# First attention reordered: score, transpose and norm work moved by one slab, key norm between a value slab's tiles

## The chip, the cores and the metric

The kernel runs on one core of a Trainium2 chip. The metric is device time in microseconds; the shown time is the median of three runs.

## The reference

Input is x (256 tokens, 1024 features). The first block is a Mamba-2 mixer, a convolutional FFN, a differential attention with 8 heads, and a second FFN. A second block (an attention over selected keys, a recurrent unit, gates and an FFN) follows. The change touches only the differential attention:

```
k, v = split(rms_norm(x, kv_ln) @ kv_w)      # k: 8 heads x 2 x 64, v: 8 heads x 128
k = rms_norm(k, k_norm) ; q = rms_norm(rms_norm(x, attn_ln) @ q_w, q_norm)
p = softmax(q k^T / 8 + bias[head], causal)  # one for each of the two halves c = 0, 1
attn = p[c=0] - lam * p[c=1]
o = rms_norm(attn @ v, subln) * (1 - lam_init)   # per head
x = x + o @ attn_out_w
```

## The kernel before

All activations stay on chip, features on the partitions. Weights stream through as slabs of 1 MB: SyncE loads a slab into one of three buffers (`raw`), ScalarE rounds it to a high part (`split_hi`, L385, called by `hi`, L1046), VectorE subtracts to get the low part (`split_lo`, L394, called by `lo`, L1424), and TensorE forms three products per tile (high x low, low x high, high x high; `mm3`, issued at L628). `hi(name)` and `lo(name)` work two slabs ahead of the one named, and `hi` waits until TensorE has finished the slab that used the same buffer. In the attention `lo` also runs an `ada` reduction (L1440) ahead of its split and another behind it; each reads a 256 KB block that GpSimd loads into one of two buffers. This is work for the second block that is placed in this stretch.

Every engine has one instruction stream, executed in order, and engines meet only at semaphores. The order of the attention is therefore written out by hand, four times, and the four have to fit: in the plan (L134), on TensorE (L915), on ScalarE (L1283) and on VectorE (L1863). The plan gives each result in PSUM a group number; group g uses bank g mod 6, and TensorE may write it (`acquire`, L358) only when the group six places earlier has been given back by its reader.

The loop variable s runs over pairs of heads: k, q and v each have four slabs, s = 0 to 3, and slab s holds heads 2s and 2s+1. The small steps of a pair are:

- `kss`, `qss`: sums of the squares of k and q per head and token (L855 to L711 on TensorE), root on ScalarE (`head_rms`, L1252), inverse on VectorE (`inverse_rms`, L1778).
- `kr`: the inverse key norm spread over the features by TensorE (`inverses`, L876, matmuls at L733) and multiplied on VectorE (`head_norm`, L1790). The query norm is a factor of the scores (`q_norm`).
- `sc`: scores of a head, two halves (L900, L901), negated with the bias and reduced to row minima on VectorE (L1811 to L1819), exponentials on ScalarE (`exps1`, L1258), combined on VectorE (`combine`, L1844 to L1856).
- `at`, `pv`: transposes of the combined map (L890), copied by ScalarE (L1271), then the product with v (L910, L912), whose square and copy ScalarE takes (L1274, L1275).
- `os`, `or`: the same norm for the output of a pair (L711, root L1252, inverse L1778, spread L733, product L1790), then its high part on ScalarE (`output_high`, L1281) and its low part on VectorE (`output_low`, L1806).

ScalarE's exponential and root need different tables, which an instruction of its own loads (ACT_TABLE_LOAD). `keep_busy(n)` (L704) issues n matmuls into a bank that nobody reads. After the last pair the output projection `ao` (four slabs) begins, whose k-th step waits for the k-th head's low part.

The order before, on TensorE, for s = 1 to 3: slab k; of earlier pairs `or`, attention 2s-3; scores 2s-2; slab q; scores 2s-1; `kss`; slab v; `kr`; two fillers; attention 2s-2; `qss`; `os`. What is left of the last pairs runs after v3 with no slab beside it.

## Time and profile before

| | us |
|---|---|
| median of three runs (1316.74 to 1323.26) | 1320.35 |
| the profiled execution's own time | 1323.19 |
| span from its first to its last instruction | 1321.1 |
| TensorE busy | 1230.6 (93%) |
| VectorE busy | 934.0 (71%) |
| ScalarE busy | 723.3 (55%) |
| GpSimd busy | 56.7 (4%) |

The mean granted TensorE clock is 0.97. A busy TensorE is not TensorE at its peak, since matmuls are pipelined. In the profile the attention lies between 475 and 613 us from the span's start: the first slab k0 starts at 467.01, k1 at 493.35, k2 at 521.53, k3 at 551.45, and the first matmul of `ao` at 612.96. A row of a timeline gives the start, the duration, the engine, the line, the operation, what it writes and reads, its shape, how many like it follow each other (x), and in brackets the idle time before it with what ended it. Durations of matmuls in such rows overlap; the distance between starts is what TensorE spends.

### The profile page before, as it was taken

How to read it: one execution, taken by the hardware profiler on the slowest of the kernel's cores; microseconds unless marked ns; L12 is line 12 of the kernel's file. 1: busy time of each engine (PE TensorE's matmuls, PEld its weight loads, DVE VectorE, ACT ScalarE, POOL GpSimd, SP SyncE). 2: the span in 40 equal slices, each digit the busy share in tenths (PEclk: the TensorE clock that was granted, in tenths of full speed). 3: DMA queues.
4: the chain of work that ended last, by engine and by line, in shares of the span. 5: the costliest groups of instructions: out<-in, count | busy, mean ns of one | idle time of the engine just before them, and what ended most of it. 6: DMA issues, size and time to landing. Idle time of an engine off the chain costs nothing.

```text
span 1321.1 us, 24735 instructions
## 1 busy us (share of the span) xinstructions
PE 1230.6 (93%) x9546; PEld 1184.6 (90%) x9546; DVE 934.0 (71%) x1686; ACT 723.3 (55%) x1073; POOL 56.7 (4%) x115
## 2 busy tenths in 40 slices
PE   6998888999999988888999999899889899999997
PEld 5998787899999988878999999899878799999997
DVE  4977987688877677665887866549755576887743
ACT  4765665365664355554666542546874436666631
POOL 1000000100001101100000001000000000000000
PEclk9899998999999999989999999899999999999999
DMA  6545453655556745522455457443322343555450
GB/s 251 179 158 173 143 204 113 230 181 173 188 183 234 257 168 189 182 97 75 167 189 188 176 207 261 171 160 108 127 85 96 128 160 128 196 186 191 151 199 32
DMA packets 38417, 220.75 MB, mean 167 GB/s; under 512 B 4943, under 2 KB 7488, under 8 KB 16960
## 3 DMA queue, kind: packets, MB, share of 16 engines
q1 hardware_dynamic: 27504, 189.97, 40.9%
q0 software_dynamic: 8112, 26.75, 5.8%
q10 hardware_dynamic: 2720, 2.90, 0.7%
q8 instruction: 57, 0.93, 0.3%
q14 instruction: 24, 0.20, 0.0%
HBM read 218.49 MB, written 1.11 MB: 166 GB/s over the span
## 4 chain that ended last, share of the span: by engine, by line
PE 62%; DVE 18%; ACT 10%; DMA 6%; issue 3%; DVEq 0%; POOL 0%; ACTq 0%
PE ps L628 56%; DMA ada_w<-in_w_ada 6%; DVE wl L399 4%; ACT wh L392 3%; DVE ada_w L1440 1%; DVE work L1474 1%; DVE xl L1468 1%; PE ps_idle L704 1%; DVE small L1819 1%; PE ps L817 1%; DVE work L1701 1%; DVE work L1813 1%; DVE work L1615 1%; DVE work L1646 1%; DVE work L1950 1%
## 5 line engine op out<-in xcount | busy, mean ns | idle before, releaser
L628 PE MATMUL ps<-xh,wl 128*128 128x256 f32 x1784 | 515.3, 289 | 13.2 <-DVE wl L399 9.8
L628 PE MATMUL ps<-xl,wh 128*128 128x256 f32 x1784 | 509.7, 286 | 0.0
L628 PE MATMUL ps<-xh,wh 128*128 128x256 f32 x1784 | 509.5, 286 | 0.0
L399 DVE TENSOR_TENSOR wl<-raw,wh 128x2048 fp32r<-128x2048 f32 (+1 forms) x178 | 400.9, 2254 | 133.9 <-ACT wh L392 133.9
L628 PEld LDWEIGHTS ps<-xh,wl 128*128 128x128 f32 x1784 | 347.8, 195 | 20.5 <-DVE wl L399 11.1
L392 ACT ACTIVATE wh<-raw 128x2048 fp32r<-128x2048 f32 (+1 forms) x178 | 333.7, 1878 | 57.5 <-PE ps L628 48.4
L628 PEld LDWEIGHTS ps<-xl,wh 128*128 128x128 f32 x1784 | 347.7, 195 | 0.5 <-issue 0.2
L628 PEld LDWEIGHTS ps<-xh,wh 128*128 128x128 f32 x1784 | 347.4, 195 | 0.0
L628 PE MATMUL ps<-actr,wh 128*128 128x256 f32 x1888 | 341.1, 283 | 0.0
L628 PEld LDWEIGHTS ps<-actr,wh 128*128 128x128 f32 x1888 | 295.0, 192 | 0.1
L628 PE MATMUL ps<-actr,wl 128*128 128x256 f32 x944 | 269.2, 285 | 7.2 <-DVE wl L399 4.7
L628 PEld LDWEIGHTS ps<-actr,wl 128*128 128x128 f32 x944 | 181.5, 192 | 10.0 <-DVE wl L399 5.9
L1586 DVE SCALAR_TENSOR_TENSOR work<-ps,vecs,work 128x255 f32<-128x255 f32 (+1 forms) x336 | 144.5, 476 | 50.7 <-ACT work L1225 41.7
L1225 ACT ACTIVATE work<-ps,vecs 128x256 f32<-128x256 f32 x132 | 74.2, 564 | 140.6 <-PE ps L628 140.3
L1057 ACT ACTIVATE work<-x 128x256 f32<-128x256 f32 x56 | 22.4, 418 | 137.0 <-DVE x L1519 42.9
L1440 DVE CUSTOM_DVE_ANT_0 ada_w<-ada_w,cact 128x512 f32<-128x512 f32 x96 | 65.2, 686 | 43.6 <-DMA ada_w<-in_w_ada 43.3
L605 POOL DMA_DIRECT2D ada_w<-in_w_ada x96 | 51.9, 541 | 748.5 <-DVE ada_sum L1440 747.6
L704 PE MATMUL ps_idle<-tri,ident 128*128 128x256 f32 x250 | 64.1, 399 | 0.0
L704 PEld LDWEIGHTS ps_idle<-tri,ident 128*128 128x128 f32 x250 | 47.0, 199 | 6.8 <-issue 1.5
L1258 ACT ACTIVATE work<-work,small 128x128 f32<-128x128 f32 (+1 forms) x48 | 21.5, 450 | 31.0 <-DVE small L1819 31.0
L1216 ACT ACTIVATE work<-work 128x256 f32<-128x256 f32 x66 | 26.6, 403 | 3.6 <-DVE work L1586 3.6
L1753 DVE TENSOR_TENSOR actr<-work,actr 128x256 f32 (+1 forms) x66 | 27.6, 419 | 0.5 <-ACT actr L1221 0.2
(252 smaller groups left out, 1045.5 us busy)
## 6 DMA issues: line engine op xcount, KB each, us to landing
raw<-in_up SPq DMA_DIRECT2D x66, 1024.0 KB, 4.9
ada_w<-in_w_ada POOLq DMA_DIRECT2D x96, 256.0 KB, 4.3
raw<-in_xbc SPq DMA_DIRECT2D x12, 1024.0 KB, 5.1
raw<-in_z SPq DMA_DIRECT2D x8, 1024.0 KB, 6.7
raw<-in_so SPq DMA_DIRECT2D x8, 1024.0 KB, 6.7
raw<-in_dn0a SPq DMA_DIRECT2D x8, 1024.0 KB, 5.5
raw<-in_dn1a SPq DMA_DIRECT2D x8, 1024.0 KB, 5.4
raw<-in_dn2a SPq DMA_DIRECT2D x8, 1024.0 KB, 4.9
```

The costliest lines, as they stand in the source:

```text
L392: nc.scalar.activation(wh[:, b % RING, 0:n], raw[:, b % RING, 0:n], ACT.Copy).then_inc(hi_done, 1)
L399: nc.vector.tensor_tensor(wl[:, b % RING, 0:n], raw[:, b % RING, 0:n], wh[:, b % RING, 0:n].bitcast(F32), ALU.subtract).then_inc(lo_done, 1)
L605: pool.dma_start(ada_w[:, a % ARING, :], io["w_ada"][a // 2][:, 512 * (a % 2):512 * (a % 2) + 512])\
L628: mm = nc.tensor.matmul(o, l, r, start=start and n == 0, stop=stop and n == 2)
L704: nc.tensor.matmul(ps_idle[:, 0:T], ident[:, :], tri[:, 0:2, :].rearrange("p a b -> p (a b)"), start=True, stop=True)
L1057: A(sq[:, m % 2, :], x[:, m, :], ACT.Square).then_inc(sq_done, 1)
L1216: A(gsil[:, (j - 1) % RING, :], pre[:, 2 * ((j - 1) % RING), :], ACT.Silu)\
L1225: A(pre[:, 2 * (j % RING) + t, :], bank(tile_group(up, j, t))[:, 0:T], ACT.Identity, scale=vdyn(f"up_w{f}", 88 + 2 * s + t), bias=vdyn(f"u ...
L1258: A(lg[:, cols], lg[:, cols], ACT.Exp, scale=-1.0, bias=mins[:, q, row + i:row + i + 1], accum_out=sums_[:, row + i:row + i + 1]).then_inc ...
L1440: V.tensor_tensor_reduce(out=w, in0=w, in1=cact[:, 512 * half:512 * half + 512], scale=1.0, scalar=0.0, op0=ALU.mult, op1=ALU.add, accum_o ...
L1586: return V.scalar_tensor_tensor(dst[:, d:T], src[:, 0:T - d], w, dst[:, d:T], ALU.mult, ALU.add)
L1753: V.tensor_tensor(dst, hbuf[:, (j - 2) % RING, :], src.bitcast(F32), ALU.subtract)\
```

## The change

It writes the four orders anew, one loop over s = 0 to 3 and a tail written out. On TensorE slab s is now: k; scores 2s-1; `os` of pair s-2; q; attention 2s-2; `kss`; `qss`; first tile of v; `kr`; second tile of v; `or` of pair s-2; attention 2s-1; scores 2s. The tail is scores 7, `os` 2, six fillers, attention 6, `or` 2, attention 7, `os` 3, two fillers, `or` 3. To place `kr` between the tiles, `stream_tok` takes a function that it calls after tile 0. The fillers inside the loop are gone, and those of the tail go from 16 to 8. ScalarE and VectorE follow in the orders of the diff; no instruction of theirs is added or removed.

```diff
@@ -131,31 +131,34 @@
     pl.stream("dn0", 12, PAIR3)
     pl.misc("n2", 2)
 
-    for s in range(6):
-        if s < 4:
-            pl.stream(f"k{s}", 1, TWO)
-        if s >= 3:
-            pl.misc(f"or{s-3}", 2)
+    for s in range(4):
+        pl.stream(f"k{s}", 1, TWO)
+        if s:
+            pl.misc(f"sc{2*s-1}", 2)
         if s >= 2:
-            pl.misc(f"at{2*s-3}")
-            pl.misc(f"pv{2*s-3}")
-        if 1 <= s < 5:
-            pl.misc(f"sc{2*s-2}", 2)
-        if s < 4:
-            pl.stream(f"q{s}", 1, TWO)
-        if 1 <= s < 5:
-            pl.misc(f"sc{2*s-1}", 2)
-        if s < 4:
-            pl.misc(f"kss{s}")
-            pl.stream(f"v{s}", 1, TWO)
-            pl.misc(f"kr{s}", 2)
-        if 1 <= s < 5:
+            pl.misc(f"os{s-2}")
+        pl.stream(f"q{s}", 1, TWO)
+        if s:
             pl.misc(f"at{2*s-2}")
             pl.misc(f"pv{2*s-2}")
-        if s < 4:
-            pl.misc(f"qss{s}")
+        pl.misc(f"kss{s}")
+        pl.misc(f"qss{s}")
+        pl.stream(f"v{s}", 1, TWO)
+        pl.misc(f"kr{s}", 2)
         if s >= 2:
-            pl.misc(f"os{s-2}")
+            pl.misc(f"or{s-2}", 2)
+        if s:
+            pl.misc(f"at{2*s-1}")
+            pl.misc(f"pv{2*s-1}")
+        pl.misc(f"sc{2*s}", 2)
+    pl.misc("sc7", 2)
+    pl.misc("os2")
+    pl.misc("at6")
+    pl.misc("pv6")
+    pl.misc("or2", 2)
+    pl.misc("at7")
+    pl.misc("pv7")
+    pl.misc("os3")
     pl.misc("or3", 2)
     pl.stream("ao", 4, TWO)
     pl.misc("n3", 2)
@@ -682,7 +685,7 @@
 
                 repeat(pe, n, stage, rolled=kind == TWO, between=between, late=late)
 
-            def stream_tok(name, X):
+            def stream_tok(name, X, between):
 
                 for s in range(PL.N[name]):
                     b = PL.S[name] + s
@@ -697,6 +700,8 @@
                                      (X[0][:, k, P * t:P * t + P], X[1][:, k, P * t:P * t + P]),
                                      k == 0, k == KD - 1, True)
                         mm.then_inc(half_done if t == 0 else slab_done, 1)
+                        if t == 0:
+                            between()
 
             def keep_busy(n):
 
@@ -912,35 +917,38 @@
                 nc.tensor.matmul(bank(g)[:, P:T], vt[:, 1, P * h:P * h + P], ATt[:, h % 2, T:384],
                                  start=False, stop=True).then_inc(misc_done, 1)
 
-            for s in range(6):
-                if s < 4:
-                    stream(f"k{s}", (xh, xl), x_ready(2) if s == 0 else None)
-                if s >= 3:
-                    inverses("or", s - 3, orms, orinv_done, 1)
+            def output_sums(s):
+                sums_by_token("os", s, o_squares, ones[:, 0:1])
+
+            def output_inverses(s):
+                inverses("or", s, orms, orinv_done, 1)
+
+            for s in range(4):
+                stream(f"k{s}", (xh, xl), x_ready(2) if s == 0 else None)
+                if s:
+                    scores(2 * s - 1)
                 if s >= 2:
-                    attend(2 * s - 3)
-                if 1 <= s < 5:
-                    scores(2 * s - 2)
-                if s < 4:
-                    stream(f"q{s}", (x2h, x2l), x_ready(3) if s == 0 else None)
-                if 1 <= s < 5:
-                    scores(2 * s - 1)
-                if s == 4:
-                    keep_busy(3)
-                if s < 4:
-                    sums_by_token("kss", s, k_squares, halves)
-                    stream_tok(f"v{s}", (xh, xl))
-                    inverses("kr", s, krms, krinv_done, 2)
-                if 1 <= s < 5:
-                    keep_busy(9 if s == 4 else 2)
+                    output_sums(s - 2)
+                stream(f"q{s}", (x2h, x2l), x_ready(3) if s == 0 else None)
+                if s:
                     attend(2 * s - 2)
-                if s < 4:
-                    sums_by_token("qss", s, q_squares, halves)
-                if s >= 4:
-                    keep_busy(2)
+                sums_by_token("kss", s, k_squares, halves)
+                sums_by_token("qss", s, q_squares, halves)
+                stream_tok(f"v{s}", (xh, xl), lambda: inverses("kr", s, krms, krinv_done, 2))
                 if s >= 2:
-                    sums_by_token("os", s - 2, o_squares, ones[:, 0:1])
-            inverses("or", 3, orms, orinv_done, 1)
+                    output_inverses(s - 2)
+                if s:
+                    attend(2 * s - 1)
+                scores(2 * s)
+            scores(7)
+            output_sums(2)
+            keep_busy(6)
+            attend(6)
+            output_inverses(2)
+            attend(7)
+            output_sums(3)
+            keep_busy(2)
+            output_inverses(3)
             stream("ao", (oh, ol), lambda k: pe.wait_ge(ol_done, k + 1))
             ffn(1, "n3", 4, 3)
 
@@ -1280,37 +1288,39 @@
                     act.wait_ge(on_done, h + 1)
                     A(oh[:, h, :], qf[:, h, :], ACT.Copy).then_inc(oh_done, 1)
 
-            for s in range(6):
-                if s < 4:
-                    kq_tiles("k", s, kf)
-                if s >= 3:
-                    output_high(s - 3)
-                if s >= 2:
-                    attend(2 * s - 3)
-                if 1 <= s < 5:
+            for s in range(4):
+                if s:
                     exps1(2 * s - 2)
-                if s < 4:
-                    kq_tiles("q", s, qf)
-                if 1 <= s < 5:
+                kq_tiles("k", s, kf)
+                if s:
                     exps1(2 * s - 1)
-                if s < 4:
-                    head_rms("kss", s, krms, 8, 64)
-                    name = f"v{s}"
-                    hi(name, 0)
-                    for t in range(2):
-                        g = PL.G[name] + t
-                        wait_tile(act, name, 0, 0, t)
-                        A(vt[:, t, 256 * s:256 * s + 256], bank(g)[:, 0:256], ACT.Copy).then_inc(vt_done, 1)
-                        act.wait_ge(vt_done, 2 * s + t + 1)
-                        act.sem_inc(free[g % PRING], 1)
-                if 1 <= s < 5:
+                kq_tiles("q", s, qf)
+                if s:
                     attend(2 * s - 2)
-                if s < 4:
-                    head_rms("qss", s, qrms, 8, 64)
                 if s >= 2:
                     head_rms("os", s - 2, orms, 4, P)
-                if s == 5:
-                    output_high(3)
+                head_rms("kss", s, krms, 8, 64)
+                head_rms("qss", s, qrms, 8, 64)
+                name = f"v{s}"
+                hi(name, 0)
+                for t in range(2):
+                    g = PL.G[name] + t
+                    wait_tile(act, name, 0, 0, t)
+                    A(vt[:, t, 256 * s:256 * s + 256], bank(g)[:, 0:256], ACT.Copy).then_inc(vt_done, 1)
+                    act.wait_ge(vt_done, 2 * s + t + 1)
+                    act.sem_inc(free[g % PRING], 1)
+                if s >= 2:
+                    output_high(s - 2)
+                if s:
+                    attend(2 * s - 1)
+            exps1(6)
+            exps1(7)
+            head_rms("os", 2, orms, 4, P)
+            attend(6)
+            output_high(2)
+            attend(7)
+            head_rms("os", 3, orms, 4, P)
+            output_high(3)
             residual("ao", 3, 4, tiles_two("ao"))
             ffn(1, "n3", [4], {}, 3, ("ao", 3))
 
@@ -1860,31 +1870,35 @@
                     else:
                         step.add(ins)
 
-            for s in range(6):
-                if s < 4:
-                    lo(f"k{s}", 0)
-                if s >= 3:
-                    head_norm("or", s - 3, qf, sgs, on_done)
-                    output_low(s - 3)
-                if 1 <= s < 5:
-                    scores(2 * s - 2)
-                if s < 4:
-                    lo(f"q{s}", 0)
-                if 1 <= s < 5:
+            def output_norm(s):
+
+                head_norm("or", s, qf, sgs, on_done)
+                output_low(s)
+
+            for s in range(4):
+                lo(f"k{s}", 0)
+                if s:
                     scores(2 * s - 1)
                     combine(2 * s - 2)
-                if s < 4:
-                    inverse_rms("kss", s, krms, krinv_done)
-                    lo(f"v{s}", 0)
-                if 1 <= s < 5:
+                lo(f"q{s}", 0)
+                if s:
                     combine(2 * s - 1)
-                if s < 4:
-                    head_norm("kr", s, kf, vec("k_norm"), kqn_done)
-                    q_norm(s)
+                lo(f"v{s}", 0)
+                inverse_rms("kss", s, krms, krinv_done)
+                q_norm(s)
                 if s >= 2:
                     inverse_rms("os", s - 2, orms, orinv_done)
-            head_norm("or", 3, qf, sgs, on_done)
-            output_low(3)
+                head_norm("kr", s, kf, vec("k_norm"), kqn_done)
+                if s >= 2:
+                    output_norm(s - 2)
+                scores(2 * s)
+            scores(7)
+            combine(6)
+            inverse_rms("os", 2, orms, orinv_done)
+            combine(7)
+            output_norm(2)
+            inverse_rms("os", 3, orms, orinv_done)
+            output_norm(3)
             residual("ao", 3, 4, tiles_two("ao"))
             ffn(1, ("n3", [(4, lambda m: vec("ffn_ln1", m), None)], 3, ("ao", 3)), 3)
```

## Rows read from the trace of the kernel before

**Rows 1.** The page: busy time, and the last chain's shares by engine.

```profile
PE 1230.6 (93%) x9546; PEld 1184.6 (90%) x9546; DVE 934.0 (71%) x1686; ACT 723.3 (55%) x1073; POOL 56.7 (4%) x115
...
PE 62%; DVE 18%; ACT 10%; DMA 6%; issue 3%; DVEq 0%; POOL 0%; ACTq 0%
```

**Rows 2.** Windows: stretch, length; busy PE, PEld, DVE, ACT, POOL (count); clock, DMA share, GB/s.

```profile
493.35:521.53 28.18, 24.51 (x205) 22.79 (x205) 19.61 (x47) 16.82 (x36) 3.23 (x6) 1.00 0.53 180
521.53:551.45 29.92, 26.79 (x220) 24.76 (x220) 21.96 (x55) 19.08 (x43) 3.95 (x7) 1.00 0.51 175
576.90:612.96 36.06, 27.47 (x152) 22.98 (x153) 18.75 (x56) 16.64 (x43) 1.17 (x2) 0.81 0.13 44
```

**Rows 3.** Timeline of TensorE, slab s=1 from q1 on.

```profile
500.12 0.38 PE L628 MATMUL ps<-actr,wl 128*128 128x256 f32 x1
...
506.07 0.50 PE L900 MATMUL ps<-work 64*128 64x128 f32 x4
...
506.93 1.05 PE L711 MATMUL ps<-blk,work 128*128 128x2 f32 x8
...
516.84 1.09 PE L733 MATMUL ps<-ident,work 128*64 128x128 f32 x16 [3.00 <-DVE work L1778]
...
517.86 1.13 PE L704 MATMUL ps_idle<-tri,ident 128*128 128x256 f32 x4
...
519.99 0.67 PE L910 MATMUL ps<-work 128*128 128x256 f32 x2 [0.67 <-ACT work L1271]
...
520.72 0.95 PE L711 MATMUL ps<-blk,work 128*128 128x2 f32 x8
```

**Rows 4.** Timeline of ScalarE, slab s=1.

```profile
506.37 1.90 ACT L392 ACTIVATE wh<-raw 128x2048 fp32r<-128x2048 f32 x1
...
509.06 0.48 ACT L1245 ACTIVATE work<-ps,vecs 128x256 f32<-128x256 f32 x1
...
514.98 1.28 ACT L1252 ACT_TABLE_LOAD   x1
...
516.28 0.27 ACT L1252 ACTIVATE work<-ps,eps_t 128x8 f32<-128x8 f32 x1
...
519.36 0.49 ACT L1271 ACTIVATE work<-ps 128x384 f32<-128x384 f32 x1 [0.23 <-PE ps L890]
...
520.92 0.38 ACT L1274 ACTIVATE work<-ps 128x256 f32<-128x256 f32 x1 [1.07 <-PE ps L912]
```

**Rows 5.** Timeline of VectorE, slab s=1.

```profile
508.30 2.29 DVE L399 TENSOR_TENSOR wl<-raw,wh 128x2048 fp32r<-128x2048 f32 x1 [2.25 <-ACT wh L392]
...
511.12 0.34 DVE L1811 SCALAR_TENSOR_TENSOR work<-ps,work 128x128 f32<-128x128 f32 x1
...
513.86 0.17 DVE L1844 RECIPROCAL small<-small 128x4 f32<-128x4 f32 x1
...
514.78 0.75 DVE L1856 SCALAR_TENSOR_TENSOR work<-work,small 128x128 f32<-128x128 f32 x2
...
516.58 0.20 DVE L1778 RECIPROCAL work<-work 128x8 f32<-128x8 f32 x1 [1.05 <-ACT work L1252]
```

**Rows 6.** Timeline, s=2: TensorE starts the slab behind scores 2; ScalarE starts a split.

```profile
530.44 0.39 PE L628 MATMUL ps<-actr,wl 128*128 128x256 f32 x1
...
534.36 1.90 ACT L392 ACTIVATE wh<-raw 128x2048 fp32r<-128x2048 f32 x1
```

**Rows 7.** Timeline of TensorE, s=3: or 0, then (attention 3, scores 4) the next slab.

```profile
558.77 1.05 PE L733 MATMUL ps<-ident,work 128*128 128x128 f32 x8
...
563.18 0.39 PE L628 MATMUL ps<-actr,wl 128*128 128x256 f32 x1
```

**Rows 8.** Timeline of VectorE: the reduction at the end of lo(v0).

```profile
494.91 0.69 DVE L1440 CUSTOM_DVE_ANT_0 ada_w<-ada_w,cact 128x512 f32<-128x512 f32 x1 [1.46 <-DMA ada_w<-in_w_ada]
```

**Rows 9.** Windows: two stretches at the lower clock, in the tail and behind k3.

```profile
583.60:593.80 10.20, 7.30 (x32) 5.70 (x32) 4.52 (x14) 3.36 (x7) 0.00 (x0) 0.50 0.28 112
552.90:556.20 3.30, 3.30 (x17) 3.30 (x17) 3.14 (x5) 0.35 (x2) 0.54 (x1) 0.50 0.45 166
```

## The prediction

> **What bounds the kernel now.** I read the page first. TensorE is busy for 93% of the span and holds 62% of the chain that ended last, VectorE 18%, ScalarE 10% [rows 1]. Everything outside the first attention keeps its order, so I went to the windows of that stage, cut at the starts of the k slabs [rows 2]. The slab loop s=1 takes 28.18 us, s=2 29.92 us, and the tail from the end of the last value slab to the start of `ao` 36.06 us, the last at a mean clock of 0.81. With s=3 up to its value slab (551.45 to 576.90, 25.45 us) the stretch from k1 to `ao` is 119.6 us. In that stretch a streamed slab is 5.95 us of TensorE (500.12 to 506.07) [rows 3], so the nine slabs from k1 on are 53.6 us; the rest is small matmuls, fillers and waits. VectorE is busy 21.96 of 29.92 us and ScalarE 19.08: neither is full. What decides is therefore the order in which three in-order queues hand work to each other. The timelines of one slab (s=1) on TensorE, ScalarE and VectorE give the price of each hand-over [rows 3 to 5].
>
> **What the change does to each queue.** Per slab the diff removes no computation. It removes two fillers in each of s=1, 2, 3 and cuts those of the tail from 16 to 8. Two fillers are a row of 1.13 us (517.86) [rows 3]: at most 3.4 us in the slabs and 4.5 us in the tail, and part of it only filled waits. It takes the attention of head 5 out of the tail. In return every slab s=1 to 3 now holds two attentions. More important are three new places in the queues:
>
> 1. VectorE: the inverse of the key norm comes behind `lo(v)`, no longer ahead of it. `lo` is an `ada` reduction, a split that waits for ScalarE's `hi(v)`, and another `ada`: from the split's start to the instruction behind it 2.82 us (508.30 to 511.12) [rows 5].
> 2. ScalarE: `hi(v)` comes behind the roots of `os`, `kss` and `qss`, and the attention copy of head 2s-2 comes behind `hi(q)` and the q tiles. Formerly `hi(v)` needed only the root of `kss`.
> 3. TensorE: the key norm's broadcast stands between the two tiles of v, so half a value slab, not a whole one, covers its wait. If VectorE is late, the second tile is late with it.
>
> **One slab worked out (s=2, t=0 at its first k matmul).** ScalarE begins `hi(k)` when the exponentials of the scores just issued are over: 3.92 us after the slab starts (530.44 to 534.36) [rows 6]. VectorE's split follows 1.93 later (506.37 to 508.30) and the next scores 2.82 after that: t=8.67. Their exponentials are over 3.86 later (511.12 to 514.98): 12.53. `hi(q)` and the q tiles take 3.07 (506.37 to just inside the end of the last copy at 509.54): 15.6 [rows 4, 5]. TensorE has had the transposes ready since 13.9, but their copy comes only now; the second product follows 0.63 after the copy starts (519.36 to 519.99): 16.25. Its square is 0.93 later (520.92), both copies about 0.56, and then ScalarE swaps to the root's table: 17.75, root of `os` at 19.05 (514.98 to 516.28 is 1.30) [rows 3, 4].
> Here the plan of PSUM banks adds a wait of its own: counted in groups of six, `qss` gets the bank of `os`, so TensorE cannot issue it until that root frees it, 19.3. `qss` costs about 0.99 up to its root, 20.3; `hi(v)` 20.45; split 22.4; inverse 25.2. TensorE's broadcast starts 0.26 later (516.58 to 516.84): 25.5. The first v tile, from 20.2, is over at 23.2, so TensorE stands for 2.3 us, where s=1 before stood for 3.00 behind the whole slab. The broadcast is 1.02 (516.84 to 517.86), the second tile half of 5.95: 29.45. Then come the broadcast of `or`, attention 2s-1 and scores 2s, the very sequence that the trace shows from 558.77 to 563.18, 4.41 us, ScalarE's two output copies included [rows 7]. The slab is 33.85 us, against 29.92. It is bound by ScalarE and VectorE in turn up to 25.5; matmuls of k and q have about a microsecond of slack.
> In s=1 there is neither `os` nor `or`: `kss` is issued at 17.0 (0.73 after the product, 519.99 to 520.72), the roots start after the table at 19.05, `hi(v)` 19.4, inverse 24.15, broadcast 24.4, second tile until 28.4, attention and scores 2.8 (4.41 less 0.9 for `or` and 0.7 for the output copies): 31.2 us.
>
> **s=0.** VectorE's two `ada` reductions per slab come faster than their loads here: the one at the end of `lo(v0)` waited for its transfer until 494.91 [rows 8], and nothing ahead of it moves. Before, the inverse stood in front of `lo(v0)`. Now it is behind: 494.91+0.61+0.12, broadcast about 495.9, second tile 496.9 to 499.9, scores 0.86 (506.07 to 506.93, rows 3): k1 starts at 500.7 instead of 493.35. The first v tile is over by about 490, so TensorE stands for some 5.7 us.
>
> **The tail.** From the end of scores 6: both last scores are now issued together, VectorE works them off by 0.17+2x2.74=5.65 (511.12 to 513.86 is one), the combination 1.65 (513.86 to the end of the pair at 514.78) and 0.2 to TensorE: transposes at 7.5. Scores, `os` and six fillers (3.4 us) last to 5.1, so TensorE stands 2.4 us. ScalarE's last exponentials end at 6.8, table and root until 8.3, copy, product 8.95, `or` 9.7, then 3.55 (the 4.41 without its scores) to 13.25, square, `os`, root 14.7, inverse 15.0, broadcast 15.3, `ao` 16.2. From the end of v3 to `ao` that is 4.4+16.2=20.6 us instead of 36.06: the tail is the good part of the change.
>
> **Sum.** 500.7+31.2+33.85+33.85=599.6, +16.2 = 615.8 for the start of `ao`, against 612.96: +2.8 us. By stretches [rows 2]: up to k1 +7.35, s=1 31.2-28.2=+3.0, s=2 33.85-29.9=+3.9, from k3 to `ao` 50.05 instead of 61.5, -11.5. What the tail gives is spent in the slabs.
> **Clock.** These are durations at the full 2.4 GHz, while the time before contains its own falls to 1.2 GHz, one of 10.2 us in the tail and shorter ones like that of 3.3 us behind k3's start [rows 9]. Inside the long one TensorE is busy only 7.30 us, with 32 records: waits and small matmuls. The new order has such stretches too: 5.7 us idle in s=0, from 13.4 to 20.2 in s=2 and s=3 little but transposes, products and two-column sums, 2.4 us idle in the tail. A fall that lands on the first v tile is hidden, since that tile waits for VectorE anyway. One that lands on broadcast, second tile and scores is not; a fall as long as the shorter one costs half of its 3.3 us, 1.7. The trace has no such slab, so its ends are 0 and 1.7 in each of three slabs. I take 1.2 for s=0, 1.5 for the three together and 1.5 in the tail, nearest to what the tail before shows: +4.2. The ends for the stage are 0 and 10. All: +7.0 us.
> `ao`, the FFN and the second block follow with the same orders and the same weights ahead; they move with it at no cost. Profiled execution: 1323.2+7.0=1330.2; that execution lies 2.8 above the median, so the median becomes 1320.35+7.0=1327.4.
>
> **Weighed against the skill.** The swap of tables: the root starts 0.02 us after the 1.28 us load ends [rows 4]. The Trainium skill, ScalarE: Activation LUTs, What ACT_TABLE_LOAD costs, says that each switch pays about 1.38 us more, to drain. By that rule the four swaps to the root, now all inside the chain, would add up to 5.5 us to the sum; the trace shows no such time, and the sum is without it.
>
> **Rivals.**
> - *The falls are covered.* TensorE has slack in k, q and the first v tile; if all falls land there, the stage ends at +0 to +3: 1320 to 1323. For it: s=1 shows a 3.00 us wait with the clock at 1.00. Against: the density of work is lower now.
> - *The order pays: faster.* If ScalarE and VectorE do not form the chain (the wait for `qss` and the table hidden, `hi(v)` early enough for the key norm), a slab is what TensorE issues: 17.9 for three slabs, 1.7 scores, 2.7 for the sums, 1.0 and 0.9 for broadcasts, 3.7 for two attentions, 27.9. That is 6 us less in each of three slabs, +7 becomes -11: 1309. It decides from the point where the key norm's inverse is ready with the end of the first v tile, 2.3 us sooner: three slabs of that cancel the +7. The order in the diff speaks against it: `lo(v)` needs `hi(v)`, that needs `qss`.
> - *The clock stays down.* As in the tail before, a fall lasts 10.2 us and takes in broadcast, tile and scores of each slab: 3.4 more in each of three slabs and 2 in s=0, +19: 1339. The Trainium skill, TensorE: Matmul & The Clock Gate, Why this matters for your kernels, warns of exactly such idle gaps between bursts of matmuls. That row s=1 kept its clock speaks for less.
> - *No effect.* The stage is reordered but the same chain of engines ends it, within 2 us: part of the first rival's time.
>
> **How the numbers follow.** About 0.5% (6.6 us) is what this kernel's measurement tells from no change; three runs lay 6.5 us apart. Forecast (+3 to +11) 0.50, falls covered 0.27, clock down 0.13, the order pays 0.10. A bit over half of the forecast case lies beyond 6.6 us, with the clock case 0.42 slower; the rest of it and the covered case are 0.48 same. The range leaves out the faster case and the far end of the last: 1318 to 1338.
>
> **What would show it.** In the profile after: k1 starts 7 us later; TensorE idles before the broadcast L733 in every value slab, released by VectorE L1778; a wait of TensorE for ScalarE's root before `qss` in s=2, 3; each of s=2, 3 about 34 us; the last scores to `ao` 16 to 18 us. If the broadcast never waits, or a slab takes under 31 us, the forecast is wrong and the time falls below the one before.

## The result

The changed kernel is slower. Its median is 1332.88 us (1330.03 to 1334.53, four runs) against 1320.73 us for the kernel before, timed beside it; the ratio is 1.0093, with a 95% interval of 1.0061 to 1.0124. That is +12.2 us, where +7.0 was forecast; the time lies in the stated range. Medians in this document leave out two executions that ran far slower, at a lower clock (1692.08 us in the fourth experiment, 1418.95 us in the sixth).

The profiled execution took 1330.03 us, with a span of 1327.9 us. Its span is only 6.8 us longer than the one before, and the reason is no part of the change: k0 starts at 463.77 us here and at 467.01 us there, although everything ahead of it is the same. In the twelve profiles of this study that start lies between 462.46 and 467.27 us. I therefore compare the stage by itself, from the start of k0 to the start of `ao`: 145.95 us before (467.01 to 612.96), 157.09 us after (463.77 to 620.86), +11.1 us. From `ao` to the end it is 708.1 us before and 707.0 after, so the whole effect lies in the stage.

### The profile page after: what moved, and what is told of

Its sections match the earlier page's. It is cut to its first block, busy times and chain, and to the rows that moved or that the text cites. A ratio compares the mean times of both kernels' runs of the same rounds, so it can differ in the third digit from the quotient of the medians.

```text
span 1327.9 us, 24679 instructions
## 1 busy us (share of the span) xinstructions
PE 1234.4 (93%) x9518; PEld 1190.1 (90%) x9518; DVE 933.7 (70%) x1686; ACT 721.9 (54%) x1073; POOL 56.5 (4%) x115
## 4 chain that ended last, share of the span: by engine, by line
PE 69%; DVE 16%; ACT 10%; issue 3%; DMA 1%; DVEq 0%; ACTq 0%
PE ps L631 62%; DVE wl L402 4%; ACT wh L395 4%; DVE work L1484 1%; DVE ada_w L1450 1%; DVE xl L1478 1%; PE ps L738 1%; PE ps_idle L709 1%; DVE small L1829 1%; PE ps L822 1%; DVE work L1711 1%; PE ps L716 1%; DMA ada_w<-in_w_ada 1%; DVE work L1823 1%; DVE work L1964 1%
## 5 line engine op out<-in xcount | busy, mean ns | idle before, releaser
L631 PE MATMUL ps<-xh,wl 128*128 128x256 f32 x1784 | 515.6, 289 | 12.2 <-DVE wl L402 9.8
L709 PE MATMUL ps_idle<-tri,ident 128*128 128x256 f32 x222 | 57.3, 401 | 0.0
L709 PEld LDWEIGHTS ps_idle<-tri,ident 128*128 128x128 f32 x222 | 42.1, 201 | 5.1 <-issue 0.3
L1266 ACT ACTIVATE work<-work,small 128x128 f32<-128x128 f32 (+1 forms) x48 | 21.5, 448 | 29.3 <-DVE small L1829 29.3
L1821 DVE SCALAR_TENSOR_TENSOR work<-ps,work 128x128 f32<-128x128 f32 x24 | 7.8, 327 | 30.8 <-PE ps L988 16.8
```

The lines of the kernel that those rows point to most:

```text
L631: mm = nc.tensor.matmul(o, l, r, start=start and n == 0, stop=stop and n == 2)
L709: nc.tensor.matmul(ps_idle[:, 0:T], ident[:, :], tri[:, 0:2, :].rearrange("p a b -> p (a b)"), start=True, stop=True)
L1266: A(lg[:, cols], lg[:, cols], ACT.Exp, scale=-1.0, bias=mins[:, q, row + i:row + i + 1], accum_out=sums_[:, row + i:row + i + 1]).then_inc ...
```

## The profile after

The page, as in [rows 1]: busy time of TensorE, and the last chain's shares.

```profile
PE 1234.4 (93%) x9518; PEld 1190.1 (90%) x9518; DVE 933.7 (70%) x1686; ACT 721.9 (54%) x1073; POOL 56.5 (4%) x115
...
PE 69%; DVE 16%; ACT 10%; issue 3%; DMA 1%; DVEq 0%; ACTq 0%
```

Busy time hardly differs (+3.8 us on TensorE); the other engines do the same work. Next the windows, as in [rows 2]: the whole stage, slabs s=1 and s=2, the end of the last value slab's stream to `ao`, the last scores to `ao`, and the stretch at the lower clock inside that.

```profile
463.77:620.86 157.09, 129.31 (x904) 119.98 (x905) 99.37 (x239) 79.84 (x180) 13.15 (x24) 0.86 0.37 128
498.01:530.67 32.66, 28.16 (x208) 26.19 (x206) 20.03 (x48) 17.55 (x40) 3.31 (x6) 0.90 0.42 146
530.67:565.48 34.81, 29.68 (x225) 27.79 (x223) 21.93 (x53) 18.64 (x43) 3.31 (x6) 0.90 0.40 136
596.30:620.86 24.56, 18.73 (x94) 15.89 (x94) 12.42 (x39) 12.31 (x34) 0.00 (x0) 0.73 0.01 3
600.54:620.86 20.32, 15.84 (x72) 13.42 (x70) 10.69 (x35) 10.06 (x29) 0.00 (x0) 0.67 0.00 1
607.60:620.80 13.20, 11.17 (x42) 9.74 (x43) 4.34 (x14) 4.64 (x11) 0.00 (x0) 0.50 0.01 1
```

Slab s=1 takes 32.66 us instead of 28.18, s=2 34.81 instead of 29.92. From the end of v3 to `ao` it is 24.56 us instead of 36.06. The granted clock (last column but two) is 0.90 in both slabs, where it was 1.00, and 0.86 over the stage, where it was 0.93. In the tail 13.2 us run at 0.50, as the stretch of 10.2 us in [rows 9].

Now slab s=2 (it starts at 530.67) on TensorE, as in [rows 3]:

```profile
546.78 0.67 PE L915 MATMUL ps<-work 128*128 128x256 f32 x2 [2.07 <-ACT work L1279]
...
547.51 0.95 PE L716 MATMUL ps<-blk,work 128*128 128x2 f32 x8
...
550.00 1.86 PE L716 MATMUL ps<-blk,work 128*128 128x2 f32 x8 [1.54 <-ACT work L1260]
...
551.72 0.56 PE L631 MATMUL ps<-wl,xh 128*128 128x256 f32 x1
...
557.07 1.09 PE L738 MATMUL ps<-ident,work 128*64 128x128 f32 x16 [0.18 <-DVE work L1788]
```

The product waits 2.07 us for ScalarE's copy of the transposes; `qss` (550.00) waits 1.54 us for the root of `os` that frees its bank, and then takes 1.72 us to the first matmul of v, instead of 0.91 at the full clock (550.56 to 551.47 in the second experiment). The first value tile takes 5.2 us (551.72 to 557.07, less the 0.18 of waiting) instead of 3.0. Behind it the broadcast L738 waits only 0.18 us. ScalarE, as in [rows 4]:

```profile
546.13 0.50 ACT L1279 ACTIVATE work<-ps 128x384 f32<-128x384 f32 x1
...
548.38 1.28 ACT L1260 ACT_TABLE_LOAD   x1
...
549.68 0.42 ACT L1260 ACTIVATE work<-ps,eps_t 128x4 f32<-128x4 f32 x2
...
551.90 0.27 ACT L1260 ACTIVATE work<-ps,eps_t 128x8 f32<-128x8 f32 x1 [1.80 <-PE ps L716]
...
552.06 1.90 ACT L395 ACTIVATE wh<-raw 128x2048 fp32r<-128x2048 f32 x1
```

The product's copy starts 15.46 us into the slab, the root of `os` at 19.01, `hi(v)` at 21.39. VectorE, as in [rows 5]: the split behind `hi(v)`, and the inverse behind it.

```profile
554.00 2.29 DVE L402 TENSOR_TENSOR wl<-raw,wh 128x2048 fp32r<-128x2048 f32 x1 [3.87 <-ACT wh L395]
...
556.82 0.26 DVE L1788 RECIPROCAL work<-work 128x8 f32<-128x8 f32 x2
```

The inverse comes 26.15 us into the slab; 25.2 was forecast. In s=0 TensorE waits longer, for the inverse behind the reduction that [rows 8] shows. VectorE's reduction, then the broadcast and the second value tile on TensorE:

```profile
490.64 0.69 DVE L1450 CUSTOM_DVE_ANT_0 ada_w<-ada_w,cact 128x512 f32<-128x512 f32 x1 [0.35 <-DMA ada_w<-in_w_ada]
...
491.50 0.91 PE L738 MATMUL ps<-ident,work 128*64 128x128 f32 x6 [2.94 <-DVE work L1788]
...
493.41 0.58 PE L631 MATMUL ps<-wl,xh 128*128 128x256 f32 x1
```

The reduction starts 26.87 us after k0, where it started 27.90 us after k0 before: its transfer came a microsecond earlier, which is no part of the change.

## Experiments

Times are medians of up to five rounds, each set beside the kernel before, 9 and 10 on another chip; "stage" is k0 to `ao` in the profile of that kernel. The changed kernel was timed in another set than the experiments, so differences against it in the medians carry the scatter of both. The stage is free of what happens ahead of it, but it is one execution of each kernel. How much that can mislead is seen in experiments 9 and 10, whose orders are the same up to the end of v1: the first tile of v1 falls on a stretch at the lower clock in one and not in the other, and slab s=1 takes 29.93 and 28.45 us. The time from k0 to the reduction that waits for its transfer at the end of `lo(v0)` differs by up to 2 us as well. A difference of one or two microseconds in the stage alone is therefore not evidence.

| kernel | median us | ratio to before (95%) | stage us |
|---|---|---|---|
| before | 1319.6 to 1320.7 | | 145.95 |
| changed | 1332.88 | 1.0093 (1.0061 to 1.0124) | 157.09 |
| 1 inverse first | 1325.27 | 1.0051 (1.0032 to 1.0071) | 152.37 |
| 2 idle matmuls | 1326.36 | 1.0058 (1.0032 to 1.0085) | 153.78 |
| 3 both | 1315.85 | 0.9972 (0.9949 to 0.9995) | 141.90 |
| 4 before, inverse late | 1341.66 | 1.0167 (1.0134 to 1.02) | 166.64 |
| 5 key norm behind v | 1327.46 | 1.0056 (1.0033 to 1.0079) | 152.62 |
| 6 as 3, `os` behind `qss` | 1317.44 | 0.9977 (0.9955 to 0.9999) | 141.87 |
| 7 as 6, copy first | 1311.83 | 0.9928 (0.9898 to 0.9959) | 136.22 |
| 8 as 7, key norm behind v | 1311.94 | 0.9941 (0.9917 to 0.9965) | 135.04 |
| 9 as 7, s=0 product first | 1312.29 | 0.9945 (0.992 to 0.9969) | 136.99 |
| 10 as 9, idle matmuls at odd heads | 1311.34 | 0.9934 (0.9911 to 0.9956) | 136.73 |

### 1. The inverse ahead of lo(v) again

```diff
+                inverse_rms("kss", s, krms, krinv_done)
                 lo(f"v{s}", 0)
-                inverse_rms("kss", s, krms, krinv_done)
                 q_norm(s)
```

> Edit to the changed kernel: VectorE forms the inverse of the key norm ahead of the split and the two reductions of lo(v), as before the change. Theory A (the late inverse is the cost of the slab loop): TensorE's idle time before the broadcast L738 goes, 2.9 us in s=0 and 0.2 to 0.6 us in s=1 to 3; k1 starts 4 us earlier, the time falls by 4 to 6 us. Theory B (the lower clock is the cost; VectorE's order is not): slabs s=1 to 3 keep 32 to 35 us, since the first value tile runs at half clock and covers the wait, and only s=0 gains. Rival C (the wait moves to the next hand-over, the copy of the transposes): no gain in any slab, within 2 us.

The median fell by 7.6 us, the stage by 4.7 us. TensorE's total waits in the stage, by what it waited for: in the changed kernel

```profile
PE ps L738 <- DVE work L1788: 4.3, 4, 2.9
...
PE ps L716 <- ACT work L1260: 3.1, 2, 1.5
```

and in this one, where the line of L738 is gone:

```profile
PE ps L905 <- issue: 1.8, 1, 1.8
...
PE ps L716 <- ACT work L1260: 2.3, 2, 1.1
```

k1 starts 30.74 us after k0 instead of 34.24: 3.5 us of the gain are in s=0. A wait of 1.8 us ahead of scores 0 is new there. The profile names no releaser for it; scores 0 need the product with the norm, which VectorE still makes behind lo(v0), and experiment 9 tests that. Slab s=2 is 33.82 us instead of 34.81. On its TensorE the inverse is now early, and yet the first value tile takes 4.35 us, not 3.0:

```profile
546.76 1.87 PE L716 MATMUL ps<-blk,work 128*128 128x2 f32 x8 [1.14 <-ACT work L1260]
...
548.49 0.56 PE L631 MATMUL ps<-wl,xh 128*128 128x256 f32 x1
...
552.84 1.09 PE L738 MATMUL ps<-ident,work 128*64 128x128 f32 x16
```

Slab s=1 is not shorter at all, 33.44 us against 32.66; 13.1 us of it are at the lower clock, where there were 6.8. So theory A is right on s=0 and B on the slabs: while the tile runs at the lower clock, an early inverse brings little.

### 2. Idle matmuls in TensorE's waits

```diff
                 transposes(f"at{h}", At[:, h % 2, :], attn_done, h + 1)
+                keep_busy(fill)
...
-                    attend(2 * s - 2)
+                    attend(2 * s - 2, 4)
                 sums_by_token("kss", s, k_squares, halves)
+                keep_busy(0 if s == 1 else 3)
                 sums_by_token("qss", s, q_squares, halves)
...
+                def key_norm():
+                    keep_busy(8 if s == 0 else 3)
+                    inverses("kr", s, krms, krinv_done, 2)
...
-            keep_busy(6)
+            keep_busy(11)
             attend(6)
```

> Edit to the changed kernel: idle matmuls (keep_busy) put into the waits of TensorE that its trace shows: 4 behind the transposes of the even head, 3 ahead of qss in s=0, 2, 3, 8 ahead of the key norm's broadcast in s=0 and 3 in the others, 11 instead of 6 in the tail. Theory A (waits for ScalarE and VectorE set the slab): the clock stays at 1.00, the first value tile takes 3 us instead of 5, but the wait behind it grows by as much; slabs s=1 to 3 shrink by at most 1.5 us each, the tail by 3 us, the whole by 3 to 7 us. Theory B (the clock is the cost): half of the 24 us by which the time at the lower clock grew comes back, 10 to 12 us, and the kernel is at the time of the one before.

Stage -3.3 us, median -6.5 us; the granted clock over the stage, the last column but two:

```profile
463.35:617.13 153.78, 134.93 (x990) 122.29 (x991) 99.26 (x239) 79.63 (x180) 13.16 (x24) 0.97 0.37 131
```

It was 0.86. The time at the lower clock fell from 44 us in six stretches to 10.2 us in three, half of which, 17 us, is the most that TensorE can have gained by it; the stage is only 3.3 us shorter. Where the rest went is in its waits and in slab s=2:

```profile
PE ps L738 <- DVE work L1795: 6.0, 3, 4.2
```

```profile
550.56 1.05 PE L716 MATMUL ps<-blk,work 128*128 128x2 f32 x8
...
551.47 0.36 PE L631 MATMUL ps<-wl,xh 128*128 128x256 f32 x1
...
556.82 1.09 PE L738 MATMUL ps<-ident,work 128*64 128x128 f32 x16 [0.93 <-DVE work L1795]
```

`qss` starts 19.33 us into the slab (550.56 less 531.23), as in the changed kernel. The tile is now quick, its fillers end at 555.9, and TensorE waits 0.93 us more for the inverse. In s=0 that wait is 4.2 us. The slab takes 34.0 us instead of 34.8. B's 10 to 12 us did not come: the tail gains 2.7 us (17.66 instead of 20.32), each of s=1 to 3 0.8 to 0.9, and s=0 is 1.8 us longer, as its broadcast starts 29.6 us after k0 instead of 27.7. VectorE's row shows why:

```profile
492.11 0.69 DVE L1457 CUSTOM_DVE_ANT_0 ada_w<-ada_w,cact 128x512 f32<-128x512 f32 x1 [1.61 <-DMA ada_w<-in_w_ada]
```

The reduction ahead of the inverse waits 1.61 us for its transfer, not 0.35, and starts 28.76 us after k0, not 26.87. Idle matmuls on TensorE need not be behind that: in the fourth experiment it starts at 28.11 and in the fifth at 28.85, both without idle matmuls added. The changed kernel's profile was lucky there. With the transfers alike the idle matmuls would gain about 5 us (an estimate, 3.3 and 1.9). This is theory A: the clock's fall and the late inverse lie side by side, and whoever takes away one finds the other.

### 3. Both

```diff
+                inverse_rms("kss", s, krms, krinv_done)
                 lo(f"v{s}", 0)
-                inverse_rms("kss", s, krms, krinv_done)
...
+                def key_norm():
+                    keep_busy(1 if s == 0 else 0)
+                    inverses("kr", s, krms, krinv_done, 2)
```

The other idle matmuls are those of the second experiment.

> Both edits together: inverse of the key norm ahead of lo(v), and the idle matmuls in TensorE's waits (none ahead of the broadcast in s=1 to 3, one in s=0). Theory A: with the clock up the first value tile ends 2 us earlier and now the inverse is there, so each slab s=1 to 3 gains about 2.3 us more than with the idle matmuls alone and s=0 5 us more; the whole lies 12 to 16 us below the changed kernel, 1 to 4 us below the one before. Theory B: no more than the idle matmuls alone plus 3 us in s=0.

Median -17.0 us, stage -15.2 us against the changed kernel. In the stage that is far more than the 4.7 and 3.3 of the two edits alone, and 2.2 us of the 7.2 more are in s=0, where the late transfer of the second experiment stands. In the medians it is less clear: 7.6 and 6.5 alone, 17.0 together, 2.9 more than their sum, which the scatter of the changed kernel's four runs could cover. Slab s=2:

```profile
546.44 1.05 PE L716 MATMUL ps<-blk,work 128*128 128x2 f32 x8
...
547.35 0.36 PE L631 MATMUL ps<-wl,xh 128*128 128x256 f32 x1
...
550.40 0.87 PE L738 MATMUL ps<-ident,work 128*64 128x128 f32 x11
```

The tile ends after 3.05 us and the broadcast follows at once. Slabs s=1 to 3 take 30.4, 31.7 and 31.9 us (32.7, 34.8 and 35.1 changed), the tail 17.5. This kernel is a little faster than the one before: its interval ends at 0.9995. It has 35 idle matmuls in the stage, though, where the kernel before has 22 and the changed one 8. The old order with idle matmuls in its own waits was not run, so it is not shown that the gain is the order's.

### 4. The inverse late in the kernel before

```diff
                 if s < 4:
-                    inverse_rms("kss", s, krms, krinv_done)
                     lo(f"v{s}", 0)
+                    inverse_rms("kss", s, krms, krinv_done)
```

> Edit to the kernel before: VectorE forms the inverse of the key norm behind lo(v) instead of ahead of it, nothing else. This measures the move of the inverse by itself. Theory A: s=0 is 4.4 us longer (the reduction that waits for its transfer until 494.9 now stands ahead of the broadcast), s=1 to 3 each 4 to 5 us (split 2.29, reduction 0.69, and ScalarE's split ahead of them), in all 14 to 20 us slower than the kernel before. Theory B: the wait is behind a whole value slab, so little of it shows, under 5 us.

Median +21.5 us, stage +20.7 us, above the upper end of theory A. In s=1 the broadcast waits not 3.00 us [rows 3] but

```profile
523.61 1.97 PE L733 MATMUL ps<-ident,work 128*64 128x128 f32 x16 [5.30 <-DVE work L1778]
```

behind a whole value slab. In s=0 it waits 4.54 us, in s=2 and 3 5.29 and 5.47, where it waited nothing, 0.67 and 0.88 us: 16 us more in all. k1 is 6.3 us later, s=1 6.8 us longer, s=2 5.5 us. The time at the lower clock doubles, from 20.5 to 41.0 us, so part of the cost comes by way of the clock.

Together with the first experiment this gives the stage for both orders: the old one takes 145.95 us with the inverse early and 166.64 with it late, the new one 152.37 and 157.09. The late inverse costs 20.7 us in the old order and only 4.7 in the new. And the new order with the inverse early is still 6.4 us slower than the old one: the late inverse alone does not explain the change's cost.

### 5. The broadcast behind the whole value slab

```diff
-                stream_tok(f"v{s}", (xh, xl), lambda: inverses("kr", s, krms, krinv_done, 2))
+                stream_tok(f"v{s}", (xh, xl), None)
+                inverses("kr", s, krms, krinv_done, 2)
```

> Edit to the changed kernel: the key norm's broadcast stands behind the whole value slab again, not between its tiles; all else as changed. If the place between the tiles is a cost because VectorE is late (theory A), the wait of 2.9 us in s=0 and 0.2 to 0.6 us in s=1 to 3 is covered by the second tile: 3 to 4.5 us less. Rival: VectorE then multiplies key norm and output norm one behind the other, ScalarE's output copies and the copy of the transposes come 0.6 to 1.2 us later in s=2 and 3, and only the 3 us of s=0 remain, or less.

Median -5.4 us, stage -4.5 us. In s=0 a wait stays:

```profile
496.99 1.09 PE L736 MATMUL ps<-ident,work 128*64 128x128 f32 x16 [2.16 <-DVE work L1787]
```

k1 is 1.5 us earlier after k0, s=1 takes 30.19 us instead of 32.66, s=2 34.86, no less. The rival is seen as well: the wait for the copy of odd heads grew from 1.34 to 1.53 us. The 2.5 us of s=1 are more than the 0.50 us that TensorE waited there, and half of them are the clock's: v1 starts 19.01 us into the slab, not 20.31, as the fall comes only with it. By this run and the eighth, the place between the tiles costs something when the inverse is late and nothing when it is early.

### 6. The output sums behind qss

```diff
         pl.misc(f"qss{s}")
+        if s >= 2:
+            pl.misc(f"os{s-2}")
         pl.stream(f"v{s}", 1, TWO)
...
-                keep_busy(0 if s == 1 else 3)
+                keep_busy(3 if s == 0 else 0)
                 sums_by_token("qss", s, q_squares, halves)
+                if s >= 2:
+                    output_sums(s - 2)
...
                 hi(name, 0)
+                if s >= 2:
+                    head_rms("os", s - 2, orms, 4, P)
```

The edit also takes away the three idle matmuls ahead of `qss` in s=2 and 3, which the expectation does not say.

> Edit to the third experiment (inverse first, idle matmuls): the output's sums os go behind qss, in the plan too, so that qss has another PSUM bank and no longer waits for the root of os; their root goes behind hi(v). Theory A (the chain over ScalarE and VectorE sets the slab, the bank is a link of it): TensorE's 1.5 us ahead of qss in s=2 and 3 go, each of the two slabs 1.0 to 1.6 us shorter, 2 to 3 us in all. Rival: the wait moves to the broadcast of the key norm (the root of kss still needs the table), the slabs stay within 0.4 us.

No gain: stage 141.87 against 141.90 us. The wait ahead of `qss` is gone, but slab s=2 (from 524.95) shows why that does not count:

```profile
538.17 0.52 PE L895 MATMUL ps<-ident,work 128*128 128x128 f32 x3 [0.40 <-DVE work L1873]
...
541.05 0.67 PE L916 MATMUL ps<-work 128*128 128x256 f32 x2 [0.63 <-ACT work L1286]
...
543.49 1.03 PE L716 MATMUL ps<-tri,work 128*128 128x1 f32 x8
...
544.38 0.46 PE L631 MATMUL ps<-wl,xh 128*128 128x256 f32 x1
```

TensorE comes to the transposes earlier and now waits for VectorE's combination there; the product starts 16.1 us into the slab as before; and v's first tile, started 0.8 us earlier in the slab than in the third experiment, fell on a stretch at the lower clock and took 4.5 us, so the slab is 0.7 us longer. Whether the fall came from the idle matmuls taken away was not separated. The stage as a whole stays the same because the tail, in which nothing was edited, ran at the full clock throughout and took 16.0 us instead of 17.5. So "no gain" is two slabs that lost and a tail that gained. My rival named the wrong next wait.

### 7. ScalarE copies the transposes ahead of the q tiles

```diff
                 hi(name, 0)
+                if then is not None:
+                    copy_map(then)
```

`copy_map` is the copy that `attend(2s-2)` began with, and is now called between `hi(q)` and the tiles of q.

> Edit to the one with os behind qss: ScalarE copies the transposes of the even head right behind hi(q), ahead of the four tile copies of q, and 2 idle matmuls instead of 4 stand in that wait. Theory A: the product starts 1.1 us earlier in each of s=1 to 3, each slab 0.7 to 1.1 us shorter, 2 to 3 us in all, the kernel 8 to 10 us below the one before. Rival: qss waits for the tile copies that are now later, or the root of kss does; no gain.

Median -5.6 us against the sixth, stage -5.7 us, where theory A said 2 to 3; 8.1 us below the kernel before. Slab s=2 (from 524.41) is 29.6 us long:

```profile
537.63 0.52 PE L895 MATMUL ps<-ident,work 128*128 128x128 f32 x3 [0.41 <-DVE work L1880]
...
539.24 0.67 PE L916 MATMUL ps<-work 128*128 128x256 f32 x2 [0.23 <-ACT work L1288]
...
541.67 1.03 PE L716 MATMUL ps<-tri,work 128*128 128x1 f32 x8
...
545.60 1.09 PE L738 MATMUL ps<-ident,work 128*64 128x128 f32 x16
...
552.33 0.67 PE L916 MATMUL ps<-work 128*128 128x256 f32 x2 [1.34 <-ACT work L1288]
```

The product starts 14.83 us into the slab instead of 16.1, `qss` no longer waits, and the tile behind it runs at the full clock (541.67+0.9 to 545.60). What is left are 0.41 us for VectorE's combination, 0.23 and 1.34 us for ScalarE's copies. Over the stage two stretches at the lower clock are left, 10.2 us. The gain beyond theory A is the clock's: s=1 and s=2 are each 2.8 us shorter, 1.3 by the earlier product and 1.5 because the first value tile takes 3.0 us and not 4.5, while s=3, where the tile still fell on a stretch at the lower clock, is 0.3 us longer. With 23 idle matmuls in the stage this kernel has one more than the kernel before; but the copy first was not tried in the old order either.

### 8. That, with the broadcast behind the value slab

```diff
-                stream_tok(f"v{s}", (xh, xl), key_norm)
+                stream_tok(f"v{s}", (xh, xl), None)
+                inverses("kr", s, krms, krinv_done, 2)
```

> Edit to that with the copy first: the key norm's broadcast behind the whole value slab. With the inverse early, theory A expects little: 1.2 us less ahead of the broadcast in s=0, within 1 us otherwise, since no wait stood there in s=1 to 3. Rival (the place between the tiles is what lets the scores follow at once): each slab 0.5 to 1.3 us longer, as the product with the norm now follows the value slab and the scores, or the output copies, wait for it.

1311.94 against 1311.83 us: no difference. In s=0 the 1.1 us of waiting ahead of the broadcast are gone as said, but TensorE waits 3.62 us ahead of scores 0 instead of 1.48. With the inverse in time the place of the broadcast is free.

### 9 and 10. What is left of the stage

```diff
+                if s == 0:
+                    head_norm("kr", s, kf, vec("k_norm"), kqn_done)
                 lo(f"v{s}", 0)
```

> Edit to the kernel with the copy first: in s=0 alone VectorE multiplies k with its norm ahead of lo(v0) instead of behind it. Theory (scores 0 wait for that product, which waits behind the reduction whose transfer is late): the 1.5 us that TensorE waits ahead of scores 0 go, k1 starts 29 us after k0 instead of 30.1, the whole 1 to 2 us less. Rival (the wait moves on: lo(v0) and q1's low part now come later, the queries' norm too): no gain, within 0.5 us.

k1 starts 28.63 us after k0 instead of 30.14, as said, and yet the median did not fall (1312.29). The wait moved to the transposes of s=1, 0.67 before:

```profile
505.62 0.52 PE L895 MATMUL ps<-ident,work 128*128 128x128 f32 x3 [1.52 <-DVE work L1880]
```

and each of s=1 to 3 had a stretch at the lower clock, where only s=3 had one in the seventh. The rival's number holds: no gain. The stretch in s=1 is not shown to be the edit's work, since the tenth kernel has the same order there and no stretch.

```diff
-                    attend(2 * s - 1)
+                    attend(2 * s - 1, 1 if s == 1 else 2)
```

> Edit to that: idle matmuls (1 in s=1, 2 in s=2 and 3) in the wait between transposes and product of the odd head, 0.8 and 1.3 us. If the falls of the clock that are left in the stage (one of 6.8 us in s=3) come from such waits, the fall goes and 1 to 2 us with it; if they come from the short matmuls of the sums, nothing changes, within 1 us.

1311.34 us, within the scatter; the stretches stay, 3.4 us each in s=2 and s=3. That of s=1 is gone, but it lay ahead of the edit. The waits of the odd heads are not what brings the others; what does was not settled.

## Why the prediction was right in direction and too small

Step by step, from the start of k0. *s=0*: forecast 7.35 us at the full clock and 1.2 for its fall; 7.9 measured (34.24 against 26.34). *Bank of `qss`, root, late inverse* (s=2): forecast product 16.25, root of `os` 19.05, `qss` 19.3; measured 16.11, 19.01 and 19.33. The chain through ScalarE and VectorE was as worked out. *Slabs*: 31.2, 33.85 and 33.85 forecast at the full clock; 32.66, 34.81 and 35.06 measured. With the clock mostly up (second experiment) they are 31.8, 34.0 and 34.2, close to that sum. *Tail*: 16.2 forecast, 20.32 measured. Of the signs named ahead, that one missed its 16 to 18 us; the late k1, the waits ahead of every broadcast, the 1.54 us ahead of `qss` in s=2 and 3 and the slabs of about 34 us came.

The full-clock sum was +2.8; the stage is +11.1, 8.3 us more. The term that was mis-sized is the clock, which I put at +4.2: by the rows below it is 8.6 to 8.8, an estimate by place, and small misses of the full-clock sum nearly cancel.

- *s=0*, forecast 1.2: the fall from 491.53 on lies on broadcast, second tile and scores, 6.51 us from the broadcast to k1 where 4.8 were forecast, 1.7 us. It shows as only 0.55 in the total, since the transfer came early and the broadcast started 27.7 us after k0, not 28.9. That is luck. The wait ahead of it was 2.9 us and not 5.7, since the first tile, too, ran at the lower clock.
- *The three slabs*, forecast 1.5: 3.6 us over the sum, nearly all of it ahead of `hi(v)`, which starts 20.65, 21.39 and 21.75 us into the slabs and not 19.4, 20.45 and 20.45. In the slabs I let a fall on the first value tile count nothing, since the tile waits anyway. That held: in s=2 the tile took 5.2 us and the wait behind it shrank from the forecast 2.3 to 0.18 us. But the fall began before the tile, on `qss`, which stands in the chain ahead of `hi(v)`: in s=2 1.90 us from its start to its root's start instead of 0.99. That is 0.9 to 1.0 us in each slab, 2.8 together. In s=1 and s=3 another 0.3 us each is exponentials that ended later than forecast.
- *The tail*, forecast 1.5: 4.1 us over the sum, all of it the clock. In the changed kernel and in the seventh experiment the transposes of head 6 start at the same place, 7.57 us after the start of the last scores (600.54 and 586.89), and there the changed kernel's fall begins:

```profile
608.11 0.88 PE L895 MATMUL ps<-ident,work 128*128 128x128 f32 x3 [2.96 <-DVE work L1866]
```

In the seventh the same tail, with five more idle matmuls in the wait ahead of the transposes, runs at the full clock:

```profile
594.46 0.52 PE L895 MATMUL ps<-ident,work 128*128 128x128 f32 x3 [0.80 <-DVE work L1880]
...
602.90 0.36 PE L631 MATMUL ps<-actr,wl 128*128 128x256 f32 x1
```

It takes 16.01 us, where 16.2 was forecast for the full clock. The same holds in the sixth; in the second and third a fall near its end leaves 17.7 and 17.5 us.

The forecast for the profiled execution, 1330.2 us, met the 1330.03 measured by accident: its stage was 4 us longer than forecast, and its k0 started 3.2 us early.

Of the rivals, "falls are covered" was wrong (the fall lands on `qss`), and "the clock stays down" was right on the tail only. "The order pays" did not come by itself, but its point of decision was the right one: once the inverse is there at the end of the first tile and the tile runs at the full clock (third experiment), the stage is 4.1 us below that of the kernel before; with the copy ahead of the q tiles 9.7 us. Both have more idle matmuls than the changed kernel, and the old order was not given the same, so that it is the order that pays is not shown. What the forecast did not say is that the two costs hide each other: 4.7 and 3.3 us alone, 15.2 us together in the stage, with the reserve on the medians made at the third experiment.

The root of `os` starts 1.30 us after the load of its table starts, in this kernel too (548.38 to 549.68), and the other three swaps to the root take 1.29 us. The drain that the Trainium skill adds to each switch (ScalarE: Activation LUTs, What ACT_TABLE_LOAD costs) is not seen here, and the sum was right to leave it out.

That the fillers removed from the loop would have prevented the falls is not shown: the idle matmuls of the experiments stand elsewhere.

## What to carry over

When work is moved between in-order queues, follow the one small instruction that another engine waits for; here an inverse of 0.2 us, moved behind a call that contains a split of 2.3 us and waits for ScalarE and a transfer, cost 20.7 us in the old order and 4.7 in the new one. The price of such a move depends on what else stands in the queues, so it has to be measured in both. Where a wait and a slow stretch lie side by side, an edit to either alone can look small: try them together before dropping the idea. A fall of the clock was free here under a tile that waits anyway, but it began on the short matmuls ahead of that tile, and there it cost 0.9 us a slab. A kernel that was given idle matmuls should be compared with an old one that was given them too.

## What the hardware showed beside that

The clock's falls in the stage came in stretches of 3.4, 6.8, 10.2 and 13.7 us. The orders alone do not fix them: kernels 9 and 10 have the same orders up to the end of v1, and only the ninth had a fall on v1's first tile, 1.5 us. In the sixth experiment every slab s=1 to 3 had a fall on its first value tile, in the seventh only s=3. The start of k0, ahead of which nothing differs, scattered over 4.8 us between executions, nearly half of the effect studied; a stage has to be compared from its own start.
